# A chunked recurrence on one Trainium2 core: two 128-token chunks with full-array matmuls, or four 64-token chunks with pairs of 64x64 array tiles

## The reference

```python
def _rwkv7_step(S, inp):
    r, w, k, v, a, b = inp
    sa = jnp.einsum('bhvk,bhk->bhv', S, a)
    S = S * w[:, :, None, :] + sa[..., None] * b[:, :, None, :] + v[..., None] * k[:, :, None, :]
    y = jnp.einsum('bhvk,bhk->bhv', S, r)
    return S, y
...
    _, y = lax.scan(_rwkv7_step, S0, seq)
...
    mean = jnp.mean(y, axis=-1, keepdims=True)
    var = jnp.mean(jnp.square(y - mean), axis=-1, keepdims=True)
    yn = ((y - mean) * lax.rsqrt(var + LNX_EPS)).reshape(B, T, D) * lnx_w + lnx_b
    bonus = (jnp.sum(rh * kh * r_k, axis=-1, keepdims=True) * vh).reshape(B, T, D)
    out = ((yn + bonus) * g).astype(x.dtype)
    return out @ w_o
```

## Time and profile before

| | us |
|---|---|
| median of 3 runs (1390.83 to 1392.82) | 1391.8 |
| the profiled execution's own time | 1392.13 |
| its span | 1390.3 |
| PE busy (98% of the span) | 1359.2 |
| DVE busy (70%) | 974.8 |
| ACT busy (47%) | 658.5 |
| POOL busy (5%) | 65.3 |

### The profile page before, as it was taken

One profiled execution on the slowest core, in us unless ns is written; L12 is line 12 of the kernel. 1 busy time (PEld: TensorE's weight loads), 2 busy tenths in 40 slices (PEclk: granted clock), 3 DMA queues, 4 the chain that ended last, 5 costly groups with the idle time before them and its releaser, 6 DMA issues.

```text
span 1390.3 us, 20468 instructions
## 1 busy us (share of the span) xinstructions
PE 1359.2 (98%) x7788; PEld 1168.6 (84%) x7788; DVE 974.8 (70%) x1701; ACT 658.5 (47%) x995; POOL 65.3 (5%) x74
## 2 busy tenths in 40 slices
PE   8999999999999999999999999999999999999999
PEld 6976999788888898888888787788888888888887
DVE  6783558687777776587777678676666697576664
ACT  4432221454444658554444567554343668454341
POOL 0003200000000002000000100000000142000000
PEclk9999999999999999999999999999999999999999
DMA  7531101465553333365554252496451423474610
GB/s 238 210 121 63 60 1 62 128 205 182 193 199 125 121 127 110 122 203 193 197 193 152 99 194 72 144 346 221 182 181 62 140 82 122 146 287 172 231 71 31
DMA packets 111100, 208.08 MB, mean 150 GB/s; under 512 B 3856, under 2 KB 53264, under 8 KB 110512
## 3 DMA queue, kind: packets, MB, share of 16 engines
q1 hardware_dynamic: 111024, 207.05, 42.6%
HBM read 205.98 MB, written 1.05 MB: 149 GB/s over the span
## 4 chain that ended last, share of the span: by engine, by line
PE 86%; DVE 7%; ACT 5%; issue 1%; POOL 0%; DMA 0%; SPq 0%; DVEq 0%; ACTq 0%; POOLq 0%
PE ps L957 21%; PE ps L932 18%; PE ps L843 11%; PE ps L937 10%; PE ps L1198 4%; PE ps L1020 2%; PE ps L995 2%; PE ps L1318 2%; PE ps L1114 2%; PE ps L908 1%; DVE Al L2413 1%; ACT Ah L1716 1%; PE ps L1361 1%; PE ps L1375 1%; ACT arena L1997 1%
## 5 line engine op out<-in xcount | busy, mean ns | idle before, releaser
L932 PE MATMUL ps<-hTx,Ah 128*128 128x512 f32 x1088 | 270.7, 391 | 0.0
L2420 DVE TENSOR_TENSOR Al<-ringA,Ah 128x2048 fp32r<-128x2048 f32 x76 | 173.9, 2288 | 103.4 <-ACT Ah L1726 103.4
L932 PEld LDWEIGHTS ps<-hTx,Ah 128*128 128x128 f32 x1088 | 199.7, 188 | 38.5
L937 PEld LDWEIGHTS ps<-hTx,Al 128*128 128x128 f32 x1152 | 156.7, 190 | 10.6
L937 PE MATMUL ps<-hTx,Al 128*128 128x256 f32 x1152 | 160.7, 282 | 0.0
L1761 ACT COPY xn<-ps 128x512 f32<-128x512 f32 x72 | 42.3, 587 | 244.2 <-PE ps L937 236.9
L1726 ACT CAST Ah<-ringA 128x2048 fp32r<-128x2048 f32 x76 | 145.8, 1918 | 16.7 <-PE ps L843 13.9
L1735 ACT CAST Bh<-ringB 128x1024 fp32r<-128x1024 f32 (+1 forms) x76 | 107.1, 1409 | 89.5 <-PE ps L957 89.5
L843 PE MATMUL ps<-Ah,hTx 128*128 128x512 f32 (+1 forms) x576 | 136.1, 387 | 1.1 <-ACT hTx L1706 0.9
L957 PE MATMUL ps<-Bh,hidh 128*128 128x512 f32 x432 | 134.9, 392 | 1.6 <-issue 1.1
L2427 DVE TENSOR_TENSOR Bl<-ringB,Bh 128x1024 fp32r<-128x1024 f32 (+1 forms) x76 | 127.0, 1671 | 10.5 <-ACT Bh L1735 10.1
(11 more groups left out here) (431 smaller groups left out, 2081.8 us busy)
## 6 DMA issues: line engine op xcount, KB each, us to landing
ringA<-in_ffn_w_in SPq DMA_DIRECT2D x44, 1024.0 KB, 7.4
ringA<-in_mlp_w SPq DMA_DIRECT2D x32, 1024.0 KB, 7.5
ringB<-in_mlp_w SPq DMA_DIRECT2D x32, 1024.0 KB, 6.8
ringB<-in_ffn_w_out SPq DMA_DIRECT2D x44, 512.0 KB, 4.1
ringA<-in_diff_w_in SPq DMA_DIRECT2D x12, 1024.0 KB, 6.4
ringA<-in_dsa_w_in SPq DMA_DIRECT2D x8, 1024.0 KB, 7.0
ringA<-in_w_k SPq DMA_DIRECT2D x4, 1024.0 KB, 7.7
ringA<-in_w_r SPq DMA_DIRECT2D x4, 1024.0 KB, 8.0
```

The costliest lines, as they stand in the source:

```text
L932: mm(o.rearrange("p (i t) -> p i t", i=2), w_hi, hTx[:, :, k * T:(k + 1) * T], start=(k == 0), stop=False)
L937: last = mm(o[:, T:2 * T], Al[:, half, k * T + j * P:k * T + j * P + P], hTh[:, k, :], start=False, stop=(k == KT - 1))
L2420: V.tensor_tensor(a_split(w, Al, half), a_half(w, (a_at[w] + par) % 2, half), a_split(w, Ah, half).bitcast(F32), ALU.subtract).then_inc(al ...
```

## The change

The recurrence has four chunks of 64 tokens. Two heads are stacked on the partitions: head `2k` on partitions 0 to 63 and head `2k + 1` on 64 to 127, everywhere in the recurrence, so that every matrix of a chunk and head is 64x64. Each product becomes a pair of matmuls, `for i in range(2): r = head_rows(i)`: one on array rows and columns 0 to 63, one on 64 to 127, with the results in the two partition halves of the same bank. A unit is now half a chunk (4 pairs of heads), so there are 8 units, `divmod(u, 2)` giving chunk and lane. The three products `M`, `MT`, `M2T` become one, `MT` (the series in 64 tokens needs no square); the steps of a unit are `nb`, `sk`, `MT`, `rhs`, `y0`, `h1`, `h2`, `h3`, `S`, `Y`. `nb` and `sk` of the next chunk stand between the steps of this one. Every chunk but the first needs the state of the chunk before it.

Around it: `block_products` are 64x64 pairs for all four chunks at once; `value_job` and `bonus_part` are in pairs of column halves; the turns of `bT` and `k2` into token order are `token_turn` (pairs of 64x64 products with the identity) for three chunks where 128x128 transposes served the first 128 tokens; `turn16("o0")` becomes `turn_tokens`; the gate products have 64 weight columns in place of 128. `E` is made by POOL (`block_inverses`), and POOL does most of the group norm of chunks 0 to 2 (`group_norm`, `with_bonus`); DVE keeps its sums, all of chunk 3 and the gates. The state of a lane is added and scaled by DVE in two operations of 128x256 (one in the first chunk), where a unit had four of 64x64. The rows `lnx_w`, `lnx_b` come in from an array of their own.

```diff
+MASKS = ["strict", "incl", "olow", "odd"]
 BLK = 16
+CH = 64
+NCK = T // CH
...
-        STEPS = [("sk", "v"), ("M", "a"), ("MT", "v"), ("M2T", "a"), ("rhs", "a"), ("y0", "a"),
-                 ("y1", "v"), ("y2", "v"), ("y3", "v"), ("U", "v"), ("sx", "v"), ("Y", "a"),
-                 ("S", "v")]
-        BANKS = {"sb": (0, 1), "sn": (0, 1), "sk": (2, 3), "M": (0,), "MT": (1,), "M2T": (1,),
-                 "rhs": (3, 0), "y0": (1,), "y1": (2,), "y2": (3,), "y3": (0,), "U": (1,),
-                 "Y": (2, 3), "S": (0,)}
-        ORDER = [(0, "sx", "v"), (1, "sx", "v")]
-        for pair in range(4):
-            us = (2 * pair, 2 * pair + 1)
-            ORDER += [(u, name, "v") for u in us for name in ("sb", "sn")]
-            ORDER += [(u + 2 if name == "sx" else u, name, e) for name, e in STEPS for u in us
-                      if (name != "S" or u < 4) and (name != "sx" or u < 6)]
-        PE_N = {(u, name): n + 1 for n, (u, name) in enumerate(
-            [(u, name) for u, name, _ in ORDER if name != "sx"])}
+        STEP_ENGINE = {"nb": "v", "sk": "v", "MT": "a", "rhs": "a", "y0": "a", "h1": "v", "h2": "v",
+                       "h3": "v", "S": "v", "Y": "a"}
+        BANKS = {"nb": 0, "MT": 0, "sk": 1, "rhs": 2, "h1": 2, "h3": 2, "S": 2, "y0": 3, "h2": 3,
+                 "Y": 3}
+        ORDER = [(l, name) for name in ("nb", "sk", "MT") for l in range(2)]
+        for c_ in range(NCK):
+            u_, more = 2 * c_, c_ < NCK - 1
+            ORDER += [(u_ + l, name) for name in ("rhs", "y0") for l in range(2)]
+            for name, then in (("h1", ("nb", 0)), ("h2", ("nb", 1)), ("h3", ("sk", 0))):
+                if more:
+                    ORDER.append((u_ + 2 + then[1], then[0]))
+                ORDER += [(u_ + l, name) for l in range(2)]
+            if more:
+                ORDER.append((u_ + 3, "sk"))
+                ORDER += [(u_ + l, "S") for l in range(2)]
+                ORDER += [(u_ + 2 + l, "MT") for l in range(2)]
+            ORDER += [(u_ + l, "Y") for l in range(2)]
+        PE_N = {step: n + 1 for n, step in enumerate(ORDER)}
...
+                for c in (2 * half, 2 * half + 1):
+                    for k in range(KT):
+                        for i in range(2):
+                            r = head_rows(i)
+                            last = mm(ps[r, c, k * CH:k * CH + CH],
+                                      fm(bT)[r, k, c * CH:c * CH + CH], AR[r, k, c, 0, :],
+                                      start=True, stop=True)
...
+            def token_turn(b, src, c):
+                for p in range(KT):
+                    for i in range(2):
+                        r = head_rows(i)
+                        last = mm(ps[r, b, p * CH:p * CH + CH], fm(src)[r, p, c * CH:c * CH + CH],
+                                  ident[r, CH * i:CH * i + CH], start=True, stop=True)
+                return last
...
+                for c2 in range(2):
+                    c = 2 * t + c2
+                    for k in range(KT):
+                        w = ringA[:, a % 2, k * 512:(k + 1) * 512].rearrange(
+                            "p (q i n) -> p q i n", q=4, i=2)
+                        if with_bonus:
+                            for q in range(2):
+                                for i in range(2):
+                                    ins = bonus_part(b2, k, 2 * c2 + q, i)
+                            if c2 and k == KT - 1:
+                                ins.then_inc(job_rdy, 1)
+                        for i in range(2):
+                            last = mm(ps[head_rows(i), b, c2 * 256:c2 * 256 + 256],
+                                      xi[:, k, c * CH:c * CH + CH], w[:, :, i, :],
+                                      start=(k == 0), stop=(k == KT - 1))
...
+            for u, name in ORDER:
+                c, l = divmod(u, 2)
+                L = lanes[l]
+                b = lane_bank(u, name)
+                MT, NB, AK = L["MT"][c % 2], L["NB"][c % 2], L["AK"][c % 2]
+                S = Sst[c % 2]
+                if name == "nb":
+                    if u >= 2:
+                        need(u - 2, "MT")
+                    elif u == 1:
+                        pe.wait_ge(job_out, J["bk"][0] + 4)
+                elif name == "MT":
+                    need(u, "nb")
+                    pe.wait_ge(wk["ex"], c + 1)
+                elif name == "rhs":
+                    need(u, "sk")
+                    if c:
+                        need(u - 2, "S")
+                    elif l == 0:
+                        pe.wait_ge(wk["btc"], 2)
+                elif name == "y0":
+                    need(u, "rhs")
+                    if c:
+                        need(u - 2, "Y")
+                elif name == "h1":
+                    need(u, "y0")
+                    need(u, "MT")
+                elif name == "h2":
+                    need(u, "h1")
+                elif name == "h3":
+                    need(u, "h2")
+                elif name in ("S", "Y"):
+                    need(u, "h3")
...
+                    elif name in ("MT", "y0", "h1", "h2", "h3"):
+                        left, right = {"MT": (NB[:, j1], E[c % 2][:, fp]),
+                                       "y0": (E[c % 2][:, fp], L["R"][:, fq]),
+                                       "h1": (MT[:, fq], L["u0"][:, fq]),
+                                       "h2": (MT[:, fq], L["ua"][:, fq]),
+                                       "h3": (MT[:, fq], L["ub"][:, fq])}[name]
                         for i in range(2):
...
+                            r = head_rows(i)
+                            last = mm(ps[r, b, fq], left[r], right[r], start=True, stop=True)
+                    elif name == "rhs":
+                        if c:
+                            for i in range(2):
+                                r = head_rows(i)
+                                mm(ps[r, b, fq], AR[r, p, c, 0, :], S[r, fp], start=True, stop=False)
+                        for i in range(2):
+                            r = head_rows(i)
+                            last = mm(ps[r, b, fq], AK[r, j0], v[r], start=(c == 0), stop=True)
...
+            def block_inverses(c):
+                pool.wait_ge(wk["nsol"], c // 2 + 1)
+                if c >= 2:
+                    pool.wait_ge(wk["mm"], PE_N[2 * c - 3, "y0"])
+                G.tensor_tensor(
+                    E[c % 2].rearrange("p (q b n) -> p q b n", q=KT, n=BLK),
+                    bc(X[:, c // 2, (c % 2) * KT:(c % 2) * KT + KT, :], 2, CH // BLK),
+                    bc(cst("blk16").rearrange("p (b n) -> p b n", n=BLK), 1, KT), ALU.mult
+                    ).then_inc(wk["ex"], 1)
+            def groups(ap):
+                return ap.rearrange("p (g v) -> p g v", v=64)
+            def with_bonus(c, dst):
+                v = chunk(vtok, c)
+                link(G.tensor_tensor(groups(dst), groups(v), bc(bon[:, 8 * c:8 * c + 8], 2, 64), ALU.mult))
+                return G.tensor_tensor(dst, dst, row("lnx_b")[:, 0:512], ALU.add)
+            def group_norm(c):
+                y = chunk(ytok, c)
+                g = gs_[:, 8 * c:8 * c + 8]
+                pool.wait_ge(wk["mean"], c + 1)
+                G.tensor_tensor(groups(y), groups(y), bc(g, 2, 64), ALU.subtract).then_inc(wk["cen"], 1)
+                link(with_bonus(c, chunk(vtok, c)))
+                pool.wait_ge(wk["rstd"], c + 1)
+                link(G.tensor_tensor(groups(y), groups(y), bc(g, 2, 64), ALU.mult))
+                link(G.tensor_tensor(y, y, row("lnx_w")[:, 0:512], ALU.mult))
+                G.tensor_tensor(y, y, chunk(vtok, c), ALU.add).then_inc(wk["yn"], 1)
...
+                if name in ("nb", "sk"):
+                    dst, m = (L["NB"], "incl") if name == "nb" else (L["AK"], "strict")
+                    last = V.copy_predicated(
+                        dst[c % 2].rearrange("p (q j t) -> p q j t", q=4, j=2), bc(mask(m, 2), 1, 4),
+                        ps[:, lane_bank(u, name), :].rearrange("p (q j t) -> p q j t", q=4, j=2))
+                elif name == "S":
+                    new = Sst[(c + 1) % 2][:, l * 256:l * 256 + 256]
+                    decay = bc(cl3[:, 4 * l:4 * l + 4, c], 2, 64)
+                    if c:
+                        link(V.tensor_tensor(L["tmp"], Sst[c % 2][:, l * 256:l * 256 + 256], p2, ALU.add))
+                        last = V.tensor_tensor(groups(new), groups(L["tmp"]), decay, ALU.mult)
+                    else:
+                        last = V.tensor_tensor(groups(new), groups(p2), decay, ALU.mult)
                 else:
...
+                    dst = {"h1": "ua", "h2": "ub", "h3": "u1"}[name]
+                    last = V.tensor_tensor(L[dst], L["u0"], p2, ALU.add)
                 last.then_inc(wk["cpv"], 1)
...
+                if (u, name) in ((3, "S"), (5, "S")):
+                    gn_mean(c - 1).then_inc(wk["mean"], 1)
+                    dve.wait_ge(wk["sqr"], c)
+                    gn_squares(c - 1)
```

(40 more changed lines are left out.)

543 lines of the change are left out of this document (217 added, 326 removed).

## The result

The changed kernel takes 1357.22 us (median of 4 runs, 1356.15 to 1358.00), the kernel before in the same session 1391.32 us (1390.15 to 1392.82): a ratio of 0.9755, 95% interval 0.9743 to 0.9767. Forecast were 1351.5 us and a range of 1341 to 1400.

What follows compares the result with a forecast made beforehand. PE instructions, paced by weight loads, were taken to bound the kernel. Recurrence -44.6, work around it +4.0 and tail +0.3 gave -40.3 us on 1392.1: 1351.8, or 1351.5 us against the median; range 1341 to 1400.

Steps and rivals of the forecast that it cites:

- The pace, 28 ns: PE, 64x64 products: a diagonal pair takes 56 ns for two instructions of 64 columns, 28 ns each.
- the 53.5 us of the recurrence's instructions: Recurrence on PE: 1664 instructions at 28 ns, 46.6 us, plus 128 at 54 ns, 6.9 us.
- Recurrence, 59.5 us: Whole recurrence: 53.5 us of instructions plus 6 us of waits, against 104.1 before, so -44.6 us.
- the 6 us added for waits: Recurrence: uncovered waits at y0 in each chunk, the masks at the start and five steps of the last chunk.
- my rival 4: Recurrence: a group-norm wait holds PE for POOL's queue, 3 to 8 us in two chunks; 1358 to 1368 us; chance 0.05.
- my rival 3: Recurrence: the clock falls to 1.2 GHz throughout, the pace doubles to 56 ns; again near 1406 us; chance 0.06.
- At nothing up to 2 us a chunk: Recurrence: cost given to POOL's late `E` and DVE's queue waiting for ACT in the group norm.
- Ahead of it, +4.0: Around the recurrence: `block_products`, `bonus_part`, `token_turn`, 448 instructions at 28 ns, 12.5 us replacing 8.5; `value_job` unchanged.
- Behind it, +0.3: Tail behind the recurrence: DVE's chain 8.8 us against 8.3 before, turns in place of eight transposes; +0.3 us in all.
- the turns behind it are 32 instructions, 0.9 us: Tail, behind DVE's last chain: 32 turn instructions on PE, 0.9 us, in place of eight transposes.
- The first: Rival on PE's pace: pairs don't overlap, or PE isn't fed faster; 56 ns an instruction, 1406 us; chance 0.17.
- The second, 33 to 49 ns: Rival on PE's pace: imperfect overlap or feeding cost; 1364 us at 35 ns, 1384 at 45; chance 0.17.

Runs made afterwards that it cites:

- the second run: The changed kernel measured again without any edit, as reference for the follow-up runs: 1356.28 us, ratio 0.9748.
- single repairs: Single edits to the changed kernel: bulk loads moved later 1355.27 us; POOL centres chunk 2 earlier 1354.99; gate products early 1355.14; group norm back on DVE 1357.07.
- all together: Changed kernel with loads, POOL order, gate products, turns, DVE gates and root-table load all moved: 1353.52 us, ratio 0.9723; first token turn to first output projection 78.12 us.

## Why the prediction was right, and where it was off

**The pace, 28 ns: right in mechanism, 1 to 2 ns small.** Measured 29.1 in the steps, 29.9 in the turns. It was worked out as half of a quarter's 56, by the weight load; one quarter has 59, two 29 to 30, four 15.8. `sk`, 54 ns forecast, has 55 (0.88/16), and a quarter of 222 is 55.5. So the 53.5 us of the recurrence's instructions are 1664 x 29.1 + 128 x 55 = 55.5.

**Recurrence, 59.5 us: measured 63.98**, and 62.76 in the second run. There PE idles for 62.76 - 57.77 = 5.0 us, and 57.8 - 55.5 = 2.3 us are products in flight with nothing behind them. So the 6 us added for waits came out at 7.3: near in size by luck, wrong in kind. What I had listed (y0, the masks, five steps of the last chunk) left about 0.6 us of idle time. The rest is the stalls for instructions (2.3 us), which I had not thought of, though 1794 instructions in 64 us stand against 961 in 104; and the group-norm wait (2.1 us), my rival 4, which is real, but falls in one chunk, the last, where no other step covers. The 1.2 us between the two runs are a fall of the clock, my rival 3 in small. "At nothing up to 2 us a chunk" held for DVE's and POOL's queues in the middle chunks.

**Ahead of it, +4.0: measured +4.5.** The recurrence starts at 143.74 instead of 139.20, in two profiles whose clock falls alike near 25 us; `block_products` take 3.88 us for 128 and the turns 5.75 for 192, 30 ns each where I had 28; `value_job` takes 7.06 as before.

**Behind it, +0.3: measured +1.5** (from 10.9, 243.3 to 254.24, to 12.38). The step "the turns behind it are 32 instructions, 0.9 us" failed. PE's queue holds all 128 turns behind the gate products, 7.02 + 3.88 + 1.49 = 12.4 us. I had followed DVE's chain alone, and counted only the last chunk's turns. (My own terms, 8.8 + 0.9 against 8.3 + 0.9, give 0.5 and not 0.3.) The sign named for it, a tail that stays near 10.7 us, was missed.

**The sum.** -40.3 forecast, -34.1 measured: 1.2 us in the tail, 0.5 ahead, 4.5 in the recurrence. The rest of the kernel moved as a block.

**The rivals.** The first is shown false: the pairs overlap, and where they are made not to, an instruction takes 59 ns and the kernel 1409 us. The rule of the Trainium skill, page "TensorEngine Tiling (Array Packing)", section "Gotcha 1: PSUM Pressure", doesn't bite here: pairs that write the two partition halves of one bank run as fast (29 ns) as with a bank each (30.2). Row tiles that write the same partitions of one bank at the same time were not tried. The second, 33 to 49 ns, is what the order of the code could have made of it.

## What to carry to other kernels

Small tiles multiply the number of instructions. Once PE's pace is a few tens of ns, look at the instruction queue's packets in the DMA view and keep bulk loads out of such a stretch; and alternate the tiles product by product. When the engine that bounds gets much faster, follow every other queue to its end, the bound engine's own too: here POOL's queue, PE's tail, DVE's last chain and the fetch lay within 2 us of each other, so single repairs showed 1 us or less each, and all together 2.8.

## What the runs showed of the hardware

An instruction of 64x64 by 64 columns costs 59 ns on one quarter, 30 on two, 15.8 on four between stalls. Instruction packets of 16 KB wait behind loads that keep the DMA engines 87% busy, and at 15 to 16 ns an instruction PE stalls for them with no load running; it goes on 2.2 to 2.8 us after a packet's start.

An elementwise DVE operation in SBUF that starts while one of POOL's 128x512 operations runs ends only behind it and takes up to 1.7 us instead of 0.69, even one of 8 columns up to 0.98 instead of 0.17; one that starts first keeps its 0.69, and POOL's takes 1.80 instead of 1.27. DVE's sums over 512 columns (0.69) and its operations that read PSUM (`h1`, 0.40 to 0.42) took no longer beside POOL than without it. The Trainium skill, page "Trainium Architecture — The Big Picture", section "🎯 What this means for kernel authors", has the port that DVE and GpSimd share as an exclusive lock, and these rows agree.

The same idle time of 2.1 us was followed by 1.2 GHz in one profile and by 2.4 GHz in the next; it was followed by 1.2 GHz behind waits of 2.7 and 1.8 us, too.
